# The output projection of a hybrid encoder layer by seven block products, with the second norm in two halves of the tokens

## What is computed

```python
def reference(x, c, w_ada, ...):
    mod = silu(c) @ w_ada[l] + b_ada[l]
    sh1, sc1, g1, sh2, sc2, g2 = split(mod, 6)
    h = rms_norm(x, norm_mix_pre[l]) * (1.0 + sc1) + sh1
    proj = h @ w_in[l]
    o_att = attention_group(aq, ak, av, q_norm[l], k_norm[l])
    o_hg = hgrn2_group(hq, hf_f, hf_b, hi, hg, hg_lower_bound, ...)
    mix = concatenate([o_att, o_hg], -1) @ w_out[l]      # the output projection
    x = x + g1 * rms_norm(mix, norm_mix_post[l])         # x1
    h = rms_norm(x, norm_ffn_pre[l]) * (1.0 + sc2) + sh2 # the second norm, h2
    y = conv_glu_ffn(h, w_up[l], conv_w[l], conv_b[l], w_down[l])
    return x + g2 * rms_norm(y, norm_ffn_post[l])
```

## Time and profile before

| | us |
|---|---|
| three runs | 2378.33, 2379.37, 2381.11 |
| median | 2379.37 |
| span of the profiled execution | 2375.8 |
| PE busy in it | 2334.7 |
| DVE busy | 1878.8 |
| ACT busy | 1104.8 |

### The profile page before, as it was taken

The page is one execution under the profiler, slowest core; times in us unless marked ns, Lnnn a source line. Parts: engine busy times, 40 slices in busy tenths (PEclk is TensorE's granted clock), DMA queues, the critical chain, the costliest instruction groups (busy, mean ns, idle before and its releaser), DMA issues.

```text
span 2375.8 us, 37218 instructions
## 1 busy us (share of the span) xinstructions
PE 2334.7 (98%) x13671; PEld 2025.8 (85%) x13671; DVE 1878.8 (79%) x2447; ACT 1104.8 (47%) x1517; POOL 128.6 (5%) x207
## 2 busy tenths in 40 slices
PE   6999999999999999999999999999999999999998
PEld 3577778888888877878999999999999998888887
DVE  5875667887777873267799999999999998888777
ACT  4266744334443353254444444444444445555554
POOL 1010000000000000000000000000000000001100
PEclk9999999999999999999999999999999999999999
DMA  9952456666666734336555555555555559779966
GB/s 366 346 157 85 133 180 208 215 219 212 207 211 198 234 89 169 98 124 159 146 140 146 145 144 143 144 142 139 141 145 145 142 176 329 251 207 285 279 226 224
DMA packets 378834, 442.47 MB, mean 186 GB/s; under 512 B 14876, under 2 KB 295716, under 8 KB 376448
## 3 DMA queue, kind: packets, MB, share of 16 engines
q1 hardware_dynamic: 359056, 369.74, 49.1%
q0 software_dynamic: 19696, 71.68, 13.0%
HBM read 418.81 MB, written 66.08 MB: 204 GB/s over the span
## 4 chain that ended last, share of the span: by engine, by line
PE 87%; DVE 5%; DMA 3%; ACT 2%; issue 2%; SPq 0%; DVEq 0%; ACTq 0%
PE bank L2132 26%; PE bank L2134 26%; PE bank L2133 26%; DMA ADA<-in_w_ada_dram 2%; PE bank L2295 2%; DVE ACC L1373 2%; DMA AB_raw<-in_w_ada_dram 1%; PE bank L2198 1%; DVE ZZ L1577 1%; PE bank L2375 1%; PE bank L2314 1%; PE bank L2189 1%; DVE W_lo L1332 0%; PE bank L2063 0%; DVE AB_acc L1636 0%
## 5 line engine op out<-in xcount | busy, mean ns | idle before, releaser
L2132 PE MATMUL bank<-H_lo,W_hi 128*128 128x256 f32 (+1 forms) x1832 | 635.7, 347 | 0.0
L2134 PE MATMUL bank<-H_hi,W_lo 128*128 128x256 f32 (+1 forms) x1832 | 613.6, 335 | 0.0
L2133 PE MATMUL bank<-H_hi,W_hi 128*128 128x256 f32 (+1 forms) x1832 | 613.2, 335 | 0.0
L2132 PEld LDWEIGHTS bank<-H_lo,W_hi 128*128 128x128 f32 x1832 | 349.3, 191 | 35.8 <-issue 6.2
L2133 PEld LDWEIGHTS bank<-H_hi,W_hi 128*128 128x128 f32 x1832 | 349.3, 191 | 35.7 <-issue 6.2
L2134 PEld LDWEIGHTS bank<-H_hi,W_lo 128*128 128x128 f32 x1832 | 348.8, 190 | 35.6
L2132 PE MATMUL bank<-T_lo,W_hi 128*128 128x256 f32 x1280 | 362.2, 283 | 0.0
L2133 PE MATMUL bank<-MGR,W_hi 128*128 128x256 f32 x1280 | 362.2, 283 | 0.0
L2134 PE MATMUL bank<-MGR,W_lo 128*128 128x256 f32 x1280 | 362.2, 283 | 0.0
L2132 PEld LDWEIGHTS bank<-T_lo,W_hi 128*128 128x128 f32 x1280 | 245.8, 192 | 0.0
L2133 PEld LDWEIGHTS bank<-MGR,W_hi 128*128 128x128 f32 x1280 | 245.8, 192 | 0.0
(11 more groups left out here) (311 smaller groups left out, 3741.7 us busy)
## 6 DMA issues: line engine op xcount, KB each, us to landing
AB_raw<-in_w_ada_dram SPq DMA_DIRECT2D x128, 512.0 KB, 4.4
UB<-in_w_up_dram SPq DMA_DIRECT2D x100, 512.0 KB, 4.1
W_raw<-in_w_in_dram SPq DMA_DIRECT2D x90, 512.0 KB, 4.8
t_dram<-in_w_down_dram POOLq DMA_DIRECT2D x88, 512.0 KB, 8.1
DRAW<-in_w_down_dram SPq DMA_DIRECT2D x66, 512.0 KB, 5.8
W_raw<-in_w_up_dram SPq DMA_DIRECT2D x56, 512.0 KB, 3.9
ADA<-in_w_ada_dram SPq DMA_DIRECT2D x48, 512.0 KB, 9.0
W_raw<-in_w_down_dram SPq DMA_DIRECT2D x44, 512.0 KB, 6.1
```

What stands on the lines that cost most here:

```text
L2132: pe.matmul(acc, st_hi, mv_lo, start=start, stop=False, skip_group_check=on)
L2133: pe.matmul(acc, st_hi, mv_hi, start=False, stop=False, skip_group_check=on)
L2134: return pe.matmul(acc, st_lo, mv_hi, start=False, stop=stop, skip_group_check=on)
```

## The change

The output projection is seen as a product of 2 x 2 blocks: 256 tokens x 1024 input rows times 1024 rows x 1024 columns. Eight block products become seven, with differences of blocks on both sides and the sums of the seven chained in the banks. In order of time the products are 1, 6 (with 7 begun), 5, 7, then 3 and 4 mixed, and 2 (the table OUT). Each has eight units; a unit has four blocks of three passes.

- Of the weights, products 1, 2 and 3 use blocks of w_out as they are. Products 5, 6 and 7 use sums that POOL's queue makes in DRAM by copies and adding transfers (out_sum): 28 of the 48 transfers stand in the attention loop behind the rotations, 20 in the heads. For product 4 DVE adds another loaded block to the loaded sum of product 6 (add_rows).
- Of the mixed outputs MX, DVE makes the differences (combine); high and low parts go to CH and CL in pieces of 256 tokens (PIECES).
- Fifteen units stand in the last head: 60 of its 80 steps have a block, 56 before. Weight loads land in five places, two before.
- ACT keeps finished sums (keep_chain), DVE adds them to other banks, and ACT writes product 1's sums back into four banks for product 2.
- The second norm is made for token tiles 2 and 3 first, while products 3 and 2 still run; PE turns their h2 between blocks of product 2. Then PE runs the 16 first up rows for these 256 tokens, and after that the 16 rows of tiles 0 and 1. The filler matmuls are gone.
- All 66 of POOL's transfers into t2_dram stand in the up projection, three for two tiles.

```diff
+OUT = ([(1, k) for k in range(8)] + [(6, k) for k in range(7)] + [(7, 0), (6, 7), (7, 1)] + [(5, k) for k in range(8)]
...
+ATTENTION_SUMS = (range(8), (8, 9), (10, 11), (12, 13), (14, 15), range(16, 24), (24, 25), (26, 27))
...
-        OUT_STEPS = [g for g in range(56) if g not in (23, 29, 35, 41, 47, 52, 53, 54)] + [57, 60, 65, 70, 73, 75, 77, 79]
+        OUT_STEPS = [g for g in range(56) if g not in (35, 41, 47, 53)] + [57, 60, 65, 70, 73, 75, 77, 79]
...
+            def out_sum(n):
+                phase, k = n // 8, n % 8
+                top, low = slice(k * P, (k + 1) * P), slice((8 + k) * P, (9 + k) * P)
+                if phase == 0:
+                    pool.dma_start(o5_dram[k], w_out[0, top, 0:1024]).then_inc(o5_landed, 16)
+                elif phase == 1:
+                    pool.wait_ge(o5_landed, o5_count + 8 * 16)
+                    pool.dma_start(o5_dram[k], w_out[0, top, 1024:2048], accum_op=ALU.add).then_inc(o5_landed, 16)
...
                 rotate(QROT[n % 2][:, :], QR[n % 4], n)
+                for m in ATTENTION_SUMS[n]:
+                    out_sum(m)
...
+            def keep_chain(dst, end):
+                act.wait_ge(unit_used, U_OUT + end)
+                for b in range(4):
+                    act.activation(dst[:, b // 2, b % 2 * 512:(b % 2 + 1) * 512], PB[CHAIN_A[b]][:, :], ACT.Copy)\
+                        .then_inc(chain_kept, 1)
...
+                if v == OUT_END[4]:
+                    for b in range(4):
+                        act.wait_ge(mg_ready, 2 + b + 1)
+                        out_square(PB[CHAIN_C[b]][:, :], 2 + b // 2, b % 2)
+                        if b % 2:
+                            mix_root(b // 2)
+                if v == OUT_END[4] + 1:
+                    for b in range(4):
+                        act.activation(PB[CHAIN_C[b]][:, :], Y_P1[:, b // 2, b % 2 * 512:(b % 2 + 1) * 512], ACT.Copy)                            .then_inc(chain_kept, 1)
+                    x1_norm(0)
+                if v == OUT_END[4] + 2:
+                    x1_norm(1)
...
+            def combine(n):
+                product, k0, k1 = PIECES[n]
...
+                if product == 7:
+                    ins = dve.tensor_tensor(a11, a11, a21, ALU.subtract)
...
+            MIX_LO_AT = {7: 2, 14: 3, 18: 4, 23: 5, 28: 6, 40: 7}
+            COMBINE_AT = {9: 3, 15: 4, 19: 5, 24: 6, 34: 7}
...
+                if v == OUT_END[4]:
+                    dve.wait_ge(unit_used, U_OUT + OUT_END[4])
+                    for b in range(4):
+                        gate_bank(CHAIN_C[b], 2 + b // 2, b % 2)
+                    sum_mix(0, 6)
+                    sum_mix(1, 8)
+                    make_x1(0, 4)
+                if v == OUT_END[4] + 1:
+                    make_x1(1, 6)
+                if v == OUT_END[4] + 2:
                     scale_x1(0)
...
+                if v == OUT_END[3]:
+                    scale_x1(1)
+                    dve.wait_ge(unit_used, U_OUT + OUT_END[3])
+                    for b in (2, 3, 0, 1):
+                        gate_bank(CHAIN_A[b], b // 2, 2 + b % 2)
...
+            sum_mix(3, 16)
             split_lo(0, 4, U_UP + 2)
...
+            make_x1(3, 14)
+            split_lo(0, 4, U_UP + 3)
+            scale_x1(2)
+            h2_low(15)
+            scale_x1(3)
...
-            def out_step(v, s):
+            def out_step(v, b):
...
+                return three_passes(bank[:, :], CH[n][:, k, t], CL[n][:, k, t], W_hi[:, slot, w], W_lo[:, slot, w],
+                                    opens and k == 0, opens and k == 7, not opens)
...
+            def turn_h2(n):
+                kt, tok = H2_ORDER[n % KT], 1 - n // KT
+                if n == 0:
+                    pe.wait_ge(mg_ready, 8)
+                    pe.wait_ge(mg_squared, 10)
+                    pe.wait_ge(x1_scaled, 2)
...
-            for n in range(SEAM_STEPS):
-                pe.matmul(PB[7][:, :], H_hi[:, n % KT, 0:P], H_hi[:, n % KT, :], start=True, stop=True)
...
+            for n in range(KT):
+                up_row(n)
+            pe.wait_ge(mg_ready, 14)
+            pe.wait_ge(mg_squared, 16)
+            for n in range(KT, 2 * KT, 2):
+                turn_h2(n)
+                turn_h2(n + 1)
+                if n >= KT + ROW_LAG:
+                    up_row(n - ROW_LAG)
+                    up_row(n - ROW_LAG + 1)
+            for n in range(2 * KT - ROW_LAG, 2 * KT):
+                up_row(n)
```

648 lines of the change are left out of this document (430 added, 218 removed).

## The result

The change made the kernel slower: 2388.28 us (median of seven runs, 2384.61 to 2398.01) against 2379.37 (seven runs, 2377.15 to 2381.86), a ratio of 1.0042 with a 95% interval of 1.003 to 1.0054. I had said 2367.

The account below looks back on a forecast made before the run. TensorE was taken to bound the kernel, busy 2334.7 of 2375.8 us. Removed 34.0 (21.8 work, 12.2 seam waiting and slow clock), added 21.8, net 12.2: from 2379.4 to 2367 us, range 2358 to 2377 (8 in 10).

Parts of the forecast that it names:

- part 7: Transfers beside attention and heads: POOL's eight copies behind the first rotation and the other moved transfers cost 0, upper end 3.
- rival C: POOL's queue beside attention delays rotation two; from 47 us for eight copies slower by over 0.2%; chance 0.08.
- The sign that I had named for C: In the trace after, a first wait longer than 2 us before 200 us would show rival C had come.
- the second layer's sums at 0: Second layer's sums moved into the up projection: POOL's queue has nothing waiting within 16 us, so 0.
- part 4: Output projection, product 4 to product 2: PE waits for norm, copies and splits on DVE and ACT, +7.9 (bounds 2.1, 12).
- part 6: Clock at row 8 in the seam: one fall to 1.2 GHz, +1.6 us (bounds 0 and four times that).
- rival B: Clock falls in each of PE's four or five gaps without fillers: 2372 to 2379 us; chance 0.22.
- part 3: End of last head: -0.3 us to unit 16, then DVE sets the pace to unit 24, +1.0 (bounds 0, 4).
- part 1: Work: 96 matmuls fewer in the output projection, 21.8 us less; 256-column first up rows add 1.0.
- part 2: Last head: DVE's added work moves the block products 5.8 later, to 891; 3.1 us lost (bounds 0, 8.1).
- part 5: Seam: PE waits 3.3 us twice at row 8, 0.9 before row 16, +7.5 in all (bounds 3, 11).
- Faster at 0.78: Chance of gaining over 4.8 us: 0.55 for the forecast, 0.15 for hidden hand-offs, 0.08 from rival B.

Follow-up runs that it names:

- e1: Changed kernel without all 48 transfers for weight sums in DRAM, products 5, 6, 7 and 4 loading plain blocks: 2379.11 us (ratio to before 0.9998).
- e2: Changed kernel without the 20 sum transfers of the heads, the 28 in attention kept: 2390.24 us (one execution).
- e9: e7 with product 4's row sums moved back and two adding transfers, not four, behind each of the last two rotations, the rest in heads: 2364.69 us.
- e12: e9 with POOL's 66 second-layer sum transfers issued two per tile over the first 33 up-projection tiles: 2363.87 us (0.9936).
- e8: Changed kernel with 42 unneeded 256-column matmuls on PE ahead of the two halves of row 8: 2381.8 us (one execution).
- e5: Changed kernel with transfers spread, and ACT and DVE reordered from unit 46 on, weight splits and bank copies ahead of norm steps: 2373.15 us (0.998).
- e11: Changed kernel with the first eight copies spread two, three, three behind three rotations, the first eight adding ones following as five and three: 2387.25 us (1.0034).
- e6: e5 with transfers placed again: 24 in the attention loop, 24 in the heads' quiet stretches: 2374.24 us (0.9973).
- e7: e5 with product 5 and 6 transfers in attention, block differences and row sums one split earlier, seam splits ahead of norm steps: 2366.54 us (0.9957).

## Why the prediction was wrong

- **The step that failed is part 7, the transfers at 0.** I looked at POOL's own queue: is the rotation late, is the sum there in time? Both were fine. The second query was not held up by its rotation, and rival C, which starts there, did not come. The sign that I had named for C, a wait longer than 2 us before 200 us, is there (2.18 on PE at 176.98), but it was a poor sign: the kernel before has such a wait too (2.02 at 169.52), and what this one goes back to is a weight. What I did not ask is what else loads at that moment. With POOL's eight copies in flight the DMA share went from 0.12 to 1.06 and one of SP's weights took 14.6 us to land; ACT splits weights in order, and PE's next work stands behind the split. Eight copies ended some 19 us after issue (158.63 to 177.78), near the 22 to 26 that I estimated, and rival C's limit of 47 us for eight was irrelevant. That estimate rests on a row read wrongly: 4.8, 7.7 and 9.6 us are the minimum, median and maximum of all 22 copies and not the landings of three. Measured, the transfers cost 9.5 us up to the last head's products (e1); the burst is 3.2 of this in the changed kernel's trace and cost up to 8.0 in others (e2). By the estimate from the Trainium skill, "DMA: Bandwidth & Descriptors", section "Anatomy of one DMA — SWDGE (gpsimd) path", that part 7 quotes the eight would have ended after some 12; the trace does not agree, and that would have changed nothing. Part 7 does not carry the miss alone: without the transfers (e1) the time is 2379.1, still above the range, and the rest lies in the terms below.
- **Also in part 7, the second layer's sums at 0.** The last stretch is 1.7 longer in this trace, and 2.7 longer in e9 than in e12, again not on POOL's queue but on a load beside it.
- **Parts 4 and 6, the waits 2.0 too high, the clock mis-sized.** Of 7.9 in part 4, 5.9 came (1.99, 1.54, 2.39; nothing at unit 50). But two falls of the clock came with them, 3.1 us, where I had charged one fall, at row 8. The bound, four falls, held; rival B's mechanism was at work with three, and for that stretch it was the better forecast. e8 shows that filling the gap ends the fall, e5 that closing the gaps at units 48 and 51 ends those two.
- **Part 3, mis-sized.** Up to unit 16 it was right: counted from the start of the last head unit 16 begins after 67.5 us, forecast 66.8. For the units up to 24 I took 1.0; units 17 to 24, with waits of 0.64 and 1.57, took 3.2 more than their matmuls. Another 1.1 lay at the row sums of product 4, to which I gave no price. With the clock and part 4 this makes 4.9 of the 6.0 us that the output projection is missing; the last 1.1 stayed open.
- **Parts 1, 2 and 5 were right.** The 96 matmuls went. From the start of the last head to its products it took 52.1 us, forecast 51.9; without late loads the last stretch is 70.6 against 64.7, 6.0 more (e1 to e5), forecast 5.8. The waits at rows 8 and 16 were 7.2, forecast 7.5; the last of them, 1.12, is a wait for ACT's h2 and not the half-width passes that I had named, so that its size came by luck. (In part 2 the terms add up to 890.9 and not to the 891.3 that I went on with.)
- **The range** had 3 us for the transfers, for the hand-offs part 3's 0 to 4 up to unit 24 and nothing from there to unit 45, so the 18.4 us were outside it. Faster at 0.78 was too sure: seven terms had been made of rows, but the two that were set to 0 had been argued from one queue alone.
- **What the idea was worth.** With the transfers, the order at the end and the second layer's sums put right the same seven products gain 15.2 us (e12), where I had forecast 12.2 for the change as it stood; that the two are near each other is no support for the forecast, since e12 has another order.

## What to carry to other kernels

A transfer whose own result is in time can still cost: it can make another queue's load late, for which an engine waits in order. When you price a moved DMA, list the loads in flight in that stretch, on every queue, and what stands behind the instruction that waits for them. Spread such transfers over stretches where few weights load, one or two at a time, adding ones above all. Where an engine both splits operands for PE and works through a norm, write the split that PE needs next ahead of the long steps of the norm, and allow for a fall of the clock (1.5 to 1.9 us each in the changed kernel) behind the gaps that are left on PE.

## What the runs showed of the hardware

- An adding transfer of 512 KB from DRAM to DRAM took POOL 0.88 to 1.78 us to issue and 8.3 to 15.2 to land, a plain copy at the same places 0.52 to 0.53 and 6.3 to 10.9 (lines L805 above), both in groups of two and four.
- The same burst of eight copies made 13.9 us into 17.2 to 22.0 in four traces, falls of the clock included, and in a fifth it cost nothing. With it spread and nothing else altered (e11) the kernel's times lay within 3.0 us instead of 13.4; but e5, e6 and e7 have it spread too, and their times lie within 9.8, 10.3 and 8.6, so it is not the only thing that widens them.
- The clock also falls where PE hardly waits. In the changed kernel two groups of eight products of one column are soon followed by matmuls at half rate:

```profile
413.22 0.95 PE L2661 MATMUL bank<-ones,AB_acc 128*128 128x1 f32 x8
414.03 0.49 PE L2418 MATMUL bank<-H_lo,W_hi 128*128 128x512 f32 x1
...
415.40 0.63 PE L2419 MATMUL bank<-H_hi,W_hi 128*128 128x512 f32 x1
415.83 0.63 PE L2420 MATMUL bank<-H_hi,W_lo 128*128 128x512 f32 x1
```

  It does so in some heads and not in the others, which have the same groups. Nor does the length of a wait tell it: behind 2.53 us of waiting at 965.62 in e7 the clock stayed, behind 1.99 at 1010.54 in the changed kernel it fell. What decides between them stayed open.
